# Down-projections of an MLP as seven half-products for each pair of blocks, weights in quarters through rings, MLPs without engine loops

## The reference

```python
D_MODEL = 1024
D_FF = 4 * D_MODEL

def rmsnorm(x, g):
    xf = x.astype(jnp.float32)
    y = xf * lax.rsqrt(jnp.mean(xf * xf, axis=-1, keepdims=True) + EPS)
    return (y * g.astype(jnp.float32)).astype(x.dtype)

def sqrelu_mlp(h, w_up, w_down):
    a = jax.nn.relu(h @ w_up)
    return (a * a) @ w_down

# in trunk, for each of the two layers, after the mixer:
x = x + sqrelu_mlp(rmsnorm(x, norm_ffn[i]), mlp_w_up[i], mlp_w_down[i])
```

## Time and profile before

| | us |
|---|---|
| median of 3 runs (2059.17 to 2065.03) | 2064.97 |
| the profiled execution | 2063.87 |
| its span, first to last instruction | 2062.1 |

### The profile page before, as it was taken

One profiled execution on the slowest core, in us unless ns is written; L12 is line 12 of the kernel. 1 busy time (PEld: TensorE's weight loads), 2 busy tenths in 40 slices (PEclk: granted clock), 3 DMA queues, 4 the chain that ended last, 5 costly groups with the idle time before them and its releaser, 6 DMA issues.

```text
span 2062.1 us, 36361 instructions
## 1 busy us (share of the span) xinstructions
PE 1973.5 (96%) x13504; PEld 1863.2 (90%) x13504; DVE 1023.9 (50%) x1727; ACT 706.8 (34%) x1133; POOL 315.5 (15%) x345
## 2 busy tenths in 40 slices
PE   5899797899999999999999999999899999999998
PEld 4878465599999999999999999999799999999998
DVE  4368684434333342345766776667543423333344
ACT  3122473233222231333555335553423313222232
POOL 3001361020000000021233333332102000000001
PEclk9999799999999999999999999999999999999999
DMA  8422202332222222222334442344332222222221
GB/s 150 108 53 65 59 1 74 101 81 72 74 72 78 75 71 76 77 72 81 91 106 120 120 130 86 112 121 120 115 102 82 72 80 72 72 81 71 72 82 72
DMA packets 309361, 176.23 MB, mean 85 GB/s; under 512 B 39776, under 2 KB 302240, under 8 KB 308256
## 3 DMA queue, kind: packets, MB, share of 16 engines
q1 hardware_dynamic: 309280, 175.11, 30.2%
HBM read 155.18 MB, written 19.72 MB: 85 GB/s over the span
## 4 chain that ended last, share of the span: by engine, by line
PE 76%; ACT 2%; DVE 1%; issue 1%; DVEq 0%; ACTq 0%
PE psum L218 68%; PE psum L688 1%; PE psum L667 1%; PE psum L681 1%; PE psum L702 1%; PE psum L685 1%; PE psum L657 1%; PE psum L645 1%; PE psum L626 0%; ACT Wm L1019 0%; DVE prev L811 0%; PE psum L638 0%; PE psum L711 0%; PE psum L1240 0%; ACT WH L196 0%
## 5 line engine op out<-in xcount | busy, mean ns | idle before, releaser
L196 ACT ACTIVATE WH<-W 128x1024 fp32r<-128x1024 f32 x218 | 230.9, 1059 | 916.0 <-PE psum L218 884.7
L218 PE MATMUL psum<-b2H,WH 128*128 128x320 f32 x1936 | 461.3, 320 | 10.0 <-DVE b2L L1227 10.0
L218 PE MATMUL psum<-b2L,WH 128*128 128x320 f32 x1936 | 446.9, 312 | 0.0
L218 PE MATMUL psum<-b2H,WL 128*128 128x320 f32 x1936 | 446.5, 312 | 0.0
L218 PE MATMUL psum<-b1H,WH 128*128 128x320 f32 (+1 forms) x1552 | 360.3, 314 | 12.6 <-DVE WL L200 6.6
L218 PE MATMUL psum<-b1L,WH 128*128 128x320 f32 (+1 forms) x1552 | 355.7, 311 | 0.0
L218 PE MATMUL psum<-b1H,WL 128*128 128x320 f32 (+1 forms) x1552 | 355.4, 310 | 0.0
L218 PEld LDWEIGHTS psum<-b2H,WH 128*128 128x128 f32 x1936 | 327.2, 191 | 17.8 <-issue 17.8
L218 PEld LDWEIGHTS psum<-b2L,WH 128*128 128x128 f32 x1936 | 329.2, 191 | 0.0
L218 PEld LDWEIGHTS psum<-b2H,WL 128*128 128x128 f32 x1936 | 329.0, 191 | 0.0
L200 DVE TENSOR_TENSOR WL<-W,WH 128x1024 fp32r<-128x1024 f32 x218 | 280.9, 1288 | 88.9 <-ACT WH L196 81.3
(11 more groups left out here) (288 smaller groups left out, 1984.3 us busy)
## 6 DMA issues: line engine op xcount, KB each, us to landing
W<-mlp_w_up SPq DMA_DIRECT2D x128, 256.0 KB, 3.1
W<-mlp_w_down SPq DMA_DIRECT2D x128, 256.0 KB, 3.0
W<-ssm_w_in SPq DMA_DIRECT2D x98, 256.0 KB, 3.1
bc<-scratch_acs SPq DMA_DIRECT2D x8, 1280.0 KB, 5.9
W<-attn_w_in SPq DMA_DIRECT2D x32, 256.0 KB, 3.7
prev<-state_ssm SPq DMA_DIRECT2D x16, 512.0 KB, 5.1
ssm_sample<-prev SPq DMA_DIRECT2D x16, 512.0 KB, 3.4
W<-ssm_w_out SPq DMA_DIRECT2D x32, 256.0 KB, 3.1
```

The costliest lines, as they stand in the source:

```text
L196: act.activation(WH[:, b.slot], W[:, b.slot], ACT.Copy).then_inc(w_hi, 1)
L218: last = pe.matmul(psum[0:m, 2 * b.slot + h, 0:TH], w[:, b.slot, k, 0:m], r[:, k, h * TH:(h + 1) * TH], start=(k == 0 and i == 0), stop=(k ...
```

## The change

Only the two MLPs and the end of the program are changed (and some semaphores share a name now). The up blocks stay as they are in PE's work: 96 matmuls for two blocks. The down blocks of a quarter are taken in pairs: blocks j and j+4 (j = 0 to 3) give the outputs of features 128j and 512+128j. Weights are split in four quarters A11, A12, A21, A22 (contraction halves by output halves, 128x512 each), and the hidden operand in B11, B12, B21, B22 (contraction halves by token halves). In place of eight half-products the pair takes seven (Winograd's form of Strassen's product), 12 matmuls each:

- products: A11·B11, S1·T1, S2·T2, S4·B22, S3·T3, A12·B21, A22·T4, in this order (numbered 0 to 6 below);
- sums of weights, 128x512 on POOL: S1 = A21+A22, S2 = S1−A11, S4 = A12−S2, S3 = A11−A21, for each pair of each quarter;
- sums of the hidden operand, 128x320 on POOL: T1, T2, T4, T3, for each of the four hidden chunks j of a quarter, made once;
- the results go into `xT` by `take` on DVE: P5 (128x640), P6, P3, P7, P2, P4 (128x320 from PSUM), U2 and U1 (128x320, both operands in SBUF), `copy_p1` on ACT (128x320), and `add_common` on POOL (128x640). P7 is the take of product 4, and `add_common` needs it.

The high and low parts are made of quarters now: `weight_hi` (ACT) and `weight_lo` (DVE) of 128x512, 4 for a pair of up blocks and 7 for a pair of down blocks. High parts go through a ring of 5 tiles, low parts through one of 6, and a sum of weights is written in the low part's place, so that S1 of the next pair can't be made before product 2 of this one is done. Raw quarters have 8 tiles. Down products use four PSUM banks in turn, so that a product needs the take of the fourth before it.

Each engine's order is written out, for all 32 pairs of a layer (numbered g; pairs 4 to 7 of 8 are down pairs). There are no loops in the MLPs.

```diff
+    DNW = ("A11", "S1", "S2", "S4", "S3", "A12", "A22")
+    DNB = (0, 1, 2, 5, 3, 4, 6)
+    def weight_sum(pool, g, s):
+        ...
+        wait_l(pool, n)
+        out = LF[l_tile(n)]
+        if s == "S1":
+            pool.tensor_tensor(out, raw_quarter(g, "A21"), raw_quarter(g, "A22"), ALU.add).then_inc(sw_sum, 1)
+    ...
+    def weight_lo(dve, n, end):
+        ...
+        elif w in ("S1", "S2"):
+            dve.wait_ge(sw_sum, 4 * downs(g) + SUMS.index(w) + 2)
+        dve.tensor_tensor(LT[l_tile(n)], weight_source(n), HT[h_tile(n)].bitcast(F32), ALU.subtract).then_inc(sw_lo, 1)
+    def down_pe(pe, g):
+        n0, first = op0(g), g % 8 == 4
+        for i in range(7):
+            ...
+            for k in range(4):
+                if first and k == 3:
+                    pe.wait_ge(h_lo, split_count(g - 1, HSEQ[1][i]))
+                for c, (w, x) in enumerate(((HT[h_tile(n)], HH), (HT[h_tile(n)], HL), (LT[l_tile(n)], HH))):
+                    last = pe.matmul(down_bank(g, i), w[:, k], x[:, DNB[i], k], start=(k == 0 and c == 0),
+                                     stop=(k == 3 and c == 2))
+    def down_dve(dve, g, end):     # j == 0 is the first down pair of a quarter, late the pairs 29 to 31
+        if j == 0:
+            relu(dve, h, "22")
+            relu(dve, h, "21")
+        else:
+            take(dve, h, "P4")
+        weight_lo(dve, n + 2, end)
+        weight_lo(dve, n + 3, end)
+        if j == 0:
+            hidden_lo(dve, h, "T2")
+        take(dve, g, "P5")
+        weight_lo(dve, n + 4, end)
+        if late:
+            next_dve(dve, layer, 2 * j - 2)
+        take(dve, g, "P6")
+        if j == 0:
+            hidden_lo(dve, h, "B22")
+        weight_lo(dve, n + 5, end)
+        take(dve, g, "P3")
+        if j == 0:
+            hidden_lo(dve, h, "T3")
+        weight_lo(dve, n + 6, end)
+        take(dve, g, "U2")
+        if late:
+            next_dve(dve, layer, 2 * j - 1)
+        take(dve, g, "P7")
+        if j == 0:
+            hidden_lo(dve, h, "B21")
+        weight_lo(dve, n + 7, end)
+        take(dve, g, "U1")
+        if j == 0:
+            hidden_lo(dve, h, "T4")
+        weight_lo(dve, n + 8, end)
+        take(dve, g, "P2")
+    def down_pool(pool, g):
+        weight_sum(pool, g, "S3")
+        if j == 0:
+            hidden_sum(pool, h, "T2")
+            hidden_sum(pool, h, "T4")
+            hidden_sum(pool, h, "T3")
+        if late:
+            chunk_pool(pool, 2 * layer + 2, 2 * j - 2)
+        if j < 3:
+            weight_sum(pool, g + 1, "S1")
+        if late:
+            chunk_pool(pool, 2 * layer + 2, 2 * j - 1)
+        add_common(pool, g)
+        if j < 3:
+            weight_sum(pool, g + 1, "S2")
+            weight_sum(pool, g + 1, "S4")
```

More of the change, by code:

```diff
@@ L208, in multiply @@
             pe.wait_ge(out_free, b.n - 1)
[L209 removed]
+        for n, k in enumerate(order):
             if ready:
[L211 removed]
+                pe.wait_ge(ready[0], ready[1] + n + 1)
             if isinstance(between, list):
[L213 to L214 removed]
+                between[n]()
+            elif between and n == 4:
                 between()
@@ L442, in mlp_pe @@
[L442 to L536, removed]
@@ new lines, in weight_source, with weight_hi @@
+    def weight_source(n):
+        w = weight(n)
+        return raw_quarter(pair_of(n), w) if w[0] == "A" else LF[l_tile(n)]
+    def weight_hi(act, n, end):
+        if n >= end:
+            return
+        g, w = pair_of(n), weight(n)
+        if w[0] == "A":
+            t, count = raw_tile(g, w)
+            act.wait_ge(sw_in[t], count)
+        else:
+            act.wait_ge(sw_sum, 4 * downs(g) + SUMS.index(w) + 1)
+        wait_h(act, n)
+        act.activation(HT[h_tile(n)], weight_source(n), ACT.Copy).then_inc(sw_hi, 1)
@@ new lines, in mlp_pe, with hidden @@
+    def mlp_pe(pe, layer):
+        for g in range(32 * layer, 32 * layer + 32):
+            if is_up(g):
+                up_pe(pe, g)
+            else:
+                down_pe(pe, g)
+    def hidden(g, what):
+        j = g % 4
+        if what == "11_12":
+            return HF[:, 0:4:3, j], out_all(0), halves(RS[:]), 2
+        if what == "21_22":
+            return HF[:, 4:6, j], out_all(1), halves(RS[:]), 4
+        h = ("21", "22").index(what)
+        return HF[:, 4 + h, j], psum[:, 2 + h, 0:TH], RS[:, h * TH:(h + 1) * TH], 4
@@ new lines, in mlp_act, with mlp_dve @@
+    def mlp_act(act, layer):
+        end = OPS * (layer + 1)
+        for g in range(32 * layer, 32 * layer + 32):
+            if is_up(g):
+                up_act(act, g, end)
+            else:
+                down_act(act, g, end)
+        next_act(act, layer, 6)
+        next_act(act, layer, 7)
+        if layer == 0:
+            act.wait_ge(sw_mm, end)
+            split_hi(act, Block(B_DT + 1), 4)
+    def mlp_dve(dve, layer):
+        end = OPS * (layer + 1)
+        for g in range(32 * layer, 32 * layer + 32):
+            if is_up(g):
+                up_dve(dve, g, end)
+            else:
+                down_dve(dve, g, end)
+        if layer:
+            next_dve(dve, layer, 6)
+        take(dve, 32 * layer + 31, "P4")
+        if not layer:
+            next_dve(dve, layer, 6)
+        next_dve(dve, layer, 7)
+        if layer == 0:
+            split_lo(dve, Block(B_DT + 1))
```

620 lines of the change are left out of this document (497 added, 123 removed).

## The result

The changed kernel is slower: 2086.43 us (median of 4 runs, 2077.81 to 2095.34) against 2062.28 us (2059.17 to 2065.03), a ratio of 1.0118 with a 95% interval of 1.0071 to 1.0165. Its profiled execution took 2086.67 us, with a span of 2084.9. The 384 matmuls are gone and took their 56.3 us with them. The span is 22.8 us longer all the same, so 79 us came back, most of it as waits of PE.

A forecast was written before the change was run, and what follows sets the result against it. PE's instruction count was taken as the MLPs' bound before the change. 2063.9 − 56.3 (matmuls) + 44.0 (first pairs) + 10.4 (plain steps) + 13.5 (late steps) = 2075.5, forecast 2076 us; own range 2061 to 2080, wide range 2022 to 2092.

The forecast's parts named there:

- rival 3: First down pairs: each wait exceeds 2 us in one piece and brings 1.2 GHz; 2084 us, up to 2095, chance 0.14.
- the clock: After T4's wait in 8 first down pairs, PE's clock may fall; taken as 0, range 0 to 8 us.
- the ends: Beginning and end of the MLPs: norm steps same in number; taken as 0, range −1 to +1.5 us.
- The removed matmuls: Down pairs, 84 matmuls instead of 96: 384 fewer over 32 pairs, saving 56.3 us.
- the loops: PE's MLP loops, now written out: no time won or lost, taken as 0.
- The exclusion carries the cost: Down pairs: DVE operations with both operands in SBUF and POOL operations wait for each other, taking turns when both are ready.
- Rivals 1 and 2: First: PE stays the bound, 2016 us, chance 0.20. Second: exclusion costs only its bare sum, 2051 us, chance 0.22.
- The first pairs: First down pair of each quarter: PE waits 5.5 us for hidden low parts; eight quarters, 44.0 us (31 to 44).
- A plain step: Between later down pairs, two in each of six quarters: 0.87 us of PE waiting each, 10.4 in all (0 to 10.4).
- The last quarter: Later steps in each layer's last quarter: 7.5 us for layer 0, 6.0 for layer 1, 13.5 together (12 to 13.5).
- Expected signs: Down pairs: PE idle for DVE's low parts, weight low parts over 0.69 us, POOL weight sums over 1.29; MLP about 458.
- Rival 1: MLPs: PE stays the bound, DVE and POOL fit in free time; 2016 us, 2008 to 2035, chance 0.20.

The follow-up runs named there:

- e_unroll: The kernel before the change with the MLP loops of PE, ACT, DVE and SyncE written out, order and sizes unchanged; 2064.83 us against 2063.12, ratio 1.0004.
- e_psum: The changed kernel, but down-pair weight low parts (except the very last pair's) subtract zeros in PSUM, so output is not the reference's; 2034.99 us.
- v3_psum: A 2043.44 us kernel whose DVE takes all read PSUM, with down-pair weight low parts also subtracting PSUM zeros (output not the reference's); 2031.5 us.
- v_banks: The changed kernel with nearly all takes reading PSUM, and the common sum one DVE operation reading P7's bank; 2056.11 us, 0.9958 of the kernel before.
- e_common: The changed kernel with the common sum moved from POOL to DVE, right behind P7's take; 2078.11 us.
- v2a: v_banks with a new order in first down pairs, and U2 moved after the weights' low part in all pairs; 2068.7 us.

## Why the prediction was right

The direction and the mechanism were right, the size was not. I forecast 2076 us with a range of its own of 2061 to 2080. The median of 2086.43 lies outside that range and a little above the upper bound of 2085 that I had summed; it is inside the wide range of 2022 to 2092, which takes in most of rival 3, and rival 3's 2084 is nearer to the measurement than my forecast. The last 7 us of that range were meant for a mis-walked first pair, and none was; that they cover the result is luck. The terms below show that the waits were walked well, and that two terms set at 0, the clock and the ends, were not 0.

- *The removed matmuls*, 56.3 us, and *the loops*, 0: as walked, shown by the table's waits and medians and by e_unroll.
- *The exclusion carries the cost*: shown by e_psum, which takes it from the weights' low parts alone, with hidden low parts and U1 still excluded, and is at 2035. Rivals 1 and 2 both needed it to cost less than walked in turns; it cost that.
- *The sizes.* The first pairs were walked as 0.8, 1.2, 3.2, 0.1 and 0.3; measured 0.45, 0.96, 3.05, 0 and small ones, in the same order T2, B22, T4, B21 and product 0. A plain step was walked as 0.87; it is 1.0. The down part of an ordinary quarter without a dip is 56.14 us, 6.86 over nominal, walked as 5.5 + 2 x 0.87 = 7.24. The last quarter of layer 0 is 13.2 over, walked as 5.5 + 7.5 = 13.0; of layer 1 10.8 (13.3 less 1.5 for twelve early transposes and 1.0 for their wait), walked as 11.5. In all 6 x 6.86 + 13.2 + 10.8 = 65.2 us, against 67.9 in the sum.
- *The clock* was taken as 0 and is 4 dips of 1.4 us (57.65 and 57.49 against 56.14; 57.63 and 57.40 against 56.09 in layer 1), 5.6 us, inside the 0 to 8 that I kept. This is the term that was mis-sized: rival 3 was half true, in 4 of 8 places. The step that failed: I set the clock at 0 because the last wait's size was uncertain, but the walk gave 3.2 us, above the 2.18 us of the earlier trace rows. Each dip also cost 1.4 us, more than the 0 to 1 that I had allowed: little of it was hidden.
- *Beginning and end* were taken as 0 (−1 to +1.5). Measured: a gap of 1.12 us at the first up product of layer 0, one of 1.71 us before the mixer's first product (line 216), and the 2.5 us of the early transposes, of which the tail gives back 0.8. About 4.5 us, outside my bound. The step that failed is the one that counted the norm's steps and saw no change because their number is the same; the profile puts the first gap down to DVE's add to x (line 413) and the second to DVE's low part of the mixer's weights (line 198), which no experiment followed.
- *The rest.* The profiled execution is 22.8 us longer than before's in span. 2.2 of it lie in code that the change does not touch (+4.6 before the first MLP, −2.4 in the mixer). The sum was 2075.5: the waits came out 2.7 lower, the clock 5.6, the ends 4.5 and untouched code 2.2 higher, 2085.1, against 2086.67 measured. The remaining 1.6 us I can't assign.
- *Expected signs*: idle time of PE by T2, B22, T4 and S2: seen. Weight low parts well over 0.69 us: 785 to 973 ns in the eight largest groups of line 1255. POOL's sums of weights over 1.29 us: 1289 to 1656 ns by group. An MLP of about 458 us: from norm sum to norm sum 463.8 in place of 452.8.

Rival 1 (PE stays the bound, 2016) was not reached by any run; v3_psum comes nearest with 2031.5.

What stays open: the four times of the changed kernel span 17.5 us, the ten of e_unroll 4.5. The runs without a profile show no clock by stretch, but each has its mean granted clock on record: 0.976 in the run of 2077.81 us, 0.971 and 0.970 in those of 2086.67 and 2086.18, 0.966 in that of 2095.34. An estimate from the dips of the profile: one of 3.41 us at half clock lowers the mean by 0.0008, so 0.010 is about 12 dips, and at 1.4 us each these are 17 us. That fits dips which come in some pairs and not in others, but where they fell was not seen, nor why their number varies.

## What to carry to other kernels

Saved matmuls are worth their count only if the operand preparation that buys them fits beside PE, and "fits" is to be counted per pair of engines, not per engine: at 65% and 33% busy, DVE and POOL together set PE's waits in the down pairs. Have DVE read one operand from PSUM wherever a product is at hand anyway (add from the bank, make partial sums in the bank); v_banks, which does this and moves two takes, came out 30 us below the changed kernel, the new order alone 16.5 and the moved common sum 8. When a queue's order is changed, look at what the same event releases on the other engine: two operations of the excluded kind released by one product's end make the later one wait for the whole of the other.

## What the runs showed of the hardware

- A DVE operation with one operand in PSUM ran at its own duration beside POOL at three sizes: 681 ns at 512 columns (e_psum), 486 at 320, 823 at 640 (v_banks). The Trainium skill's section cited above says the same of the lock; the rows of the first down pair of the changed kernel add that with work queued on both engines they took turns, operation by operation.
- DVE adding into a PSUM bank in place (P7's bank + U2, 0.48 to 0.50 us) is no slower than writing to SBUF (0.49).
- The clock's fall does not follow from the length of PE's wait alone. In the changed kernel it fell after 3.05 us in 4 of 8 first pairs. In e_common PE waited 3.61 us before 903.37 and the clock stayed at full speed:

```profile
899.00:903.00 4.00, 0.92 (x7) 0.66 (x5) 3.96 (x5) 1.02 (x2) 3.02 (x2) 1.00 0.64 183
903.40:906.40 3.00, 3.00 (x20) 3.00 (x21) 2.92 (x6) 0.96 (x3) 0.00 (x0) 1.00 0.00 0
```

  In the last quarter of layer 1 of e_common it did fall, after a shorter wait of 2.91 us that ended at 2045.05:

```profile
2041.00:2045.00 4.00, 1.30 (x9) 1.04 (x8) 3.96 (x6) 0.63 (x1) 1.79 (x2) 1.00 0.00 0
2045.30:2048.60 3.30, 3.30 (x14) 3.30 (x14) 2.70 (x6) 0.11 (x1) 0.00 (x0) 0.50 0.00 0
```

  In v2a it fell once in the MLPs, at 903.75, after waits of 1.07 and 1.90 us close together. What tells these apart was not settled.
